# The second pass's activation blocks loaded from ScalarE's DMA queue instead of SyncE's

## The reference, cut to what matters

```python
mod = silu(c) @ ada_w + ada_b; shift, scale, gate = split(mod, 3)
h = rms_norm(x, norm_pre) * (1 + scale) + shift        # 1024 x 2048
q, k, v, z = h @ w_in                                  # 2048 x 8192, 8 heads x 256 columns each
p = softmax(mask(q k^T * scale))                       # two maps of 128 columns a head
attn = p[0] - lam * p[1]
o = rms_norm(attn @ v, subln) * (1 - lambda_init) * silu(z)
out = x + gate * rms_norm(o @ w_out, norm_post)
```

## Time and profile before

| | us |
|---|---|
| median of 3 runs | 2010.06 |
| lowest, highest | 2008.69, 2011.51 |
| the profiled execution's own time | 2007.15 |
| its span in the profile | 2005.2 |

### The profile page before, as it was taken

One profiled execution on the slowest core, in us unless ns is written; L12 is line 12 of the kernel. 1 busy time (PEld: TensorE's weight loads), 2 busy tenths in 40 slices (PEclk: granted clock), 3 DMA queues, 4 the chain that ended last, 5 costly groups with the idle time before them and its releaser, 6 DMA issues.

```text
span 2005.2 us, 26598 instructions
## 1 busy us (share of the span) xinstructions
PE 1940.0 (97%) x9252; PEld 1587.8 (79%) x9252; DVE 1277.7 (64%) x2096; ACT 785.8 (39%) x1567; POOL 566.1 (28%) x624
## 2 busy tenths in 40 slices
PE   3989999999999999999999999999999999999998
PEld 1358888888888887888888888888888878888886
DVE  1456766666655544787888888878888755434352
ACT  4433333333444332344444444444444433322240
POOL 1023333423365522433243423233242310000000
PEclk9999999999999999999999999999999999999999
DMA  9658666664365767786867778776867685476553
GB/s 301 208 179 263 211 191 216 199 203 141 134 213 197 260 243 262 231 243 201 254 207 231 229 222 255 211 238 201 253 208 242 213 291 169 132 255 200 161 154 85
DMA packets 391489, 426.52 MB, mean 213 GB/s; under 512 B 21078, under 2 KB 287420, under 8 KB 388796
## 3 DMA queue, kind: packets, MB, share of 16 engines
q1 hardware_dynamic: 391072, 424.76, 66.6%
q10 hardware_dynamic: 284, 0.05, 0.0%
HBM read 294.70 MB, written 130.03 MB: 212 GB/s over the span
## 4 chain that ended last, share of the span: by engine, by line
PE 90%; DVE 3%; issue 2%; DMA 2%; POOL 1%; ACT 1%; SPq 1%; DVEq 0%; POOLq 0%; ACTq 0%
PE ps L1544 28%; PE ps L1546 27%; PE ps L1545 27%; PE ps L1532 3%; PE ps L1664 2%; SPq L475 1%; PE ps L1638 1%; PE ps L1520 1%; POOL stg L736 1%; POOL sums L723 1%; DMA w_raw<-in_diff_w_out_dram 1%; PE ps L1683 1%; DVE ring L1109 1%; DMA h_dr<-stg 0%; DVE cc_low L1268 0%
## 5 line engine op out<-in xcount | busy, mean ns | idle before, releaser
L1544 PE MATMUL ps<-blk,ring 128*128 128x512 f32 x1536 | 608.7, 396 | 12.1 <-ACT cc L888 5.3
L1546 PE MATMUL ps<-blk,ring 128*128 128x512 f32 x1536 | 600.6, 391 | 0.0
L1545 PE MATMUL ps<-blk,ring 128*128 128x512 f32 x1536 | 600.5, 391 | 0.0
L1544 PEld LDWEIGHTS ps<-blk,ring 128*128 128x128 f32 x1536 | 289.8, 189 | 72.0 <-issue 13.5
L1546 PEld LDWEIGHTS ps<-blk,ring 128*128 128x128 f32 x1536 | 289.6, 189 | 61.7
L1545 PEld LDWEIGHTS ps<-blk,ring 128*128 128x128 f32 x1536 | 289.8, 189 | 57.1
L1109 DVE TENSOR_TENSOR ring<-sums,ring 128x512 fp32r<-128x512 f32 x256 | 225.4, 881 | 128.3 <-ACT ring L819 126.0
L723 POOL TENSOR_TENSOR sums<-raw 128x512 f32<-128x512 f32 x128 | 192.6, 1505 | 386.5 <-DVE ring L1109 287.0
L819 ACT ACTIVATE ring<-sums 128x512 fp32r<-128x512 f32 x256 | 160.0, 626 | 177.8 <-PE ps L1546 177.8
L1109 DVE TENSOR_TENSOR ring<-raw,ring 128x512 fp32r<-128x512 f32 x192 | 161.5, 842 | 83.4 <-ACT ring L819 82.5
L723 POOL TENSOR_TENSOR sums<-sums,raw 128x512 f32<-128x512 f32 x128 | 189.8, 1482 | 25.5 <-DVE ring L1109 18.4
(11 more groups left out here) (152 smaller groups left out, 3017.2 us busy)
## 6 DMA issues: line engine op xcount, KB each, us to landing
raw<-in_diff_w_in_dram SPq DMA_DIRECT2D x64, 1024.0 KB, 7.2
d_dr<-cc SPq DMA_DIRECT2D x128, 256.0 KB, 2.8
cc<-d_dr SPq DMA_DIRECT2D x128, 256.0 KB, 4.0
w_raw<-in_diff_w_out_dram SPq DMA_DIRECT2D x128, 256.0 KB, 3.6
ada<-in_ada_w_dram SPq DMA_DIRECT2D x108, 256.0 KB, 4.0
ada<-in_ada_w_dram SPq DMA_DIRECT2D x32, 512.0 KB
q_sb<-q_dr SPq DMA_DIRECT2D x64, 256.0 KB, 3.2
k_sb<-k_dr SPq DMA_DIRECT2D x64, 256.0 KB, 4.0
```

What stands on the lines that cost most here:

```text
L1544: MM(dst, a_hi, b_hi, start=start, stop=False, skip_group_check=True)
L1545: MM(dst, a_hi, b_lo, start=False, stop=False, skip_group_check=True)
L1546: return MM(dst, a_lo, b_hi, start=False, stop=stop, skip_group_check=True)
```

## The change

The seven `load_blk` calls move from SP's list into ACT's, at the same n, with the same waits and semaphores. In ACT's list they stand at the end of an iteration, behind `first_out(n - 1)` and `high_w(n + 3)`.

```diff
         @block.sync
-            def load_blk(op):
-
-                if op < 2:
-                    for e in range(2):
-                        sp.wait_ge(stg_st[e], 16 * 14)
-                    sp.wait_ge(xT_mm, 32)
-                else:
-                    sp.wait_ge(prod, NA - NP + op - 1)
-                sp.dma_start(slotB[op][:, :, :, :].bitcast(F32), h_dr[op]).then_inc(blk_in[op], 16)
             for n in range(NA):
...
-                if n in (NA - 22, NA - 20):
-                    load_blk((n - NA + 22) // 2)
-                if n > NA - 6:
-                    load_blk(n - NA + 7)
                 if NA - 3 <= n < NA - 1:
                     load_partial(GP, (C11, C12)[n - NA + 3])
...
         @block.scalar
+            def load_blk(op):
+
+                if op < 2:
+                    for e in range(2):
+                        act.wait_ge(stg_st[e], 16 * 14)
+                    act.wait_ge(xT_mm, 32)
+                else:
+                    act.wait_ge(prod, NA - NP + op - 1)
+                act.dma_start(slotB[op][:, :, :, :].bitcast(F32), h_dr[op]).then_inc(blk_in[op], 16)
+
             for n in range(NA):
...
                 if 0 <= j < 4 and 4 <= r < 4 + NP:
                     high_blk(j * NP + r - 4)
+                if n in (NA - 22, NA - 20):
+                    load_blk((n - NA + 22) // 2)
+                if n > NA - 6:
+                    load_blk(n - NA + 7)
```

## The result

The changed kernel takes 2013.76 us (median of 22 runs, 2010.17 to 2017.81), the one before 2009.38 (22 runs, 2006.03 to 2012.01). The ratio is 1.0022 with a 95% interval of 1.0016 to 1.0028: 4.4 us slower, just over the 0.2% that the prediction set as its bound for a change that can be told. The profiled execution took 2017.81 us with a span of 2015.6, which is 4 us over the median of its kind. That is 10.4 us more than the profiled execution of before: 2.1 us before product 224, 5.0 from product 224 to 230, and 3.3 behind it, of which 2.6 lie between 1600 and 1640 us, far from the change.

A forecast was written before the change was run, and what follows sets the result against it. TensorE, 97% busy, was taken to lose time only to waits and lowered clock at the turn of the passes. Packets one for one add 3.4 us to 2007.15: 2010.6, or 2013.5 on the median's scale; range 2006.4 to 2017.5.

The forecast's parts named there:

- What bounds the kernel: TensorE is busy 97%; at the turn of the passes late partials cost 4.85 us of waits and 3.4 of clock.
- Seven issues hidden on ACT: Seven block issues on ACT at 0.44 us each, 3.1 us in all, fit its idle time before splits.
- The start near 732.2: ACT issues block 2 behind the split at 731.50, 3.5 us later than SP's 728.72.
- Blocks 0 and 1 cost nothing: Issued 22 and 21 products before they are read, they cost nothing even if their loads take twice as long.
- SP is no longer held: C12's load can be issued near 740, not 744.9, seemingly gaining 5 us if the data then moves.
- Does it move?: Two queues on full DMA engines: bytes shared equally lands C12 near 744, packets one for one, the end taken, near 765.
- The other end: DMA engines share bytes equally between queues: SP's transfers get 212 GB/s and are through by 743.
- The sum: With packets one for one, C12 lands 764.8, product 228 starts 765.7, product 230 3.4 us later than before; chance 42%.
- rival 2: C22's load, behind stores and reads again, lands 4 us later: 3.5 us more, 2017.0; chance 20%.
- The first: Engines share by bytes, both waits go, product 230 waits for block 6: 2006.4 to 2008.1, say 2007.1; chance 22%.
- The third: ACT is held 7.9 us at blocks 5 and 6, as SP was: end 2014 to 2015; chance 6%.
- The fourth: A few small packets, say four, pass per large one; C12 near 757, within 2 us of before; chance 10%.

The follow-up runs named there:

- the first experiment: The changed kernel with blocks 2 to 6 back in SyncE's list, only blocks 0 and 1 issued by ScalarE; ratio to the kernel before 1.0002 (0.9992 to 1.0012).

## Why the prediction was right

*What bounds the kernel*: right. The cost that can be traced to the change appeared where a partial was late at the turn of the passes.

*Seven issues hidden on ACT*: right, 0.33 us each and no hold. The start near 732.2 was late by 0.7: with the 2.1 us of this execution taken off it was 731.5, since an issue goes out beside the split and not behind it.

*Blocks 0 and 1 cost nothing*: right, by the profile of the first experiment.

*SP is no longer held*: C12's load was issued at 742.3, not near 740, since product 218's store took 10.2 us to land beside the blocks. Nothing hung on it, for C12 stood behind raw.

*Does it move?* This was the choice that decided, and the end taken, packets one for one, holds: 271 to 272. The other end, bytes shared equally, is excluded by that row and by the runs of 4 KB. The evidence that the prediction had was thin: one instruction fetch of 0.99 us, which is less than 1.24 but also more than the 0.62 of a block's packet. It had to be set against other fetches: those of 16 KB on q8 in the trace of before take 0.88 us at the least and 1.02 in the median, so this one was hardly slowed. The prediction did not make that comparison, and one packet is little; in part it was luck. The Trainium skill's rule (DMA: Bandwidth & Descriptors, section Queues, rings and completion order), a round at packet granularity, agrees with the trace in that; its turns of some 9 to 17 descriptors do not, for a turn here was a single packet, by the 264 of 271 above. The same page's sentence that several issuing engines save only issue time (section Issuing engines are not separate DMA queues) did not hold here: the change also altered which transfers got through first, and that is what cost time.

*The sum*, with 2.1 us taken off: C12 landed at 766.1 where 764.8 was reckoned, 228 started at 767.0 (765.7), C22 was issued at 766.8 and landed 2.6 later (766.1 and 2.8), and the turn grew by 5.0 us in the profile, 4.4 in the medians, where 3.4 was forecast with 2.9 to 4.8 as the forecast's own range: the profile is just over it, the medians are in it. Two terms were undersized. C12 landed 1.3 us later: raw landed at 765.4, where its packets were reckoned to be through by 763.1. The sum took all 16 DMA engines alike. Of raw's 1024 packets 986 had started by 765.0, which is 762.9 and as reckoned, but the last ended at 767.2, and the landing followed that one; from 762.5 to 763.5 ten packets of blocks were still in the traffic. And 228 took 22.13 to 27.39 us of the turn, 5.26, at the lowered clock, not 4.57. Product 229 with its transposes took 3.34, which is 0.3 less than the 3.4 forecast implies. The chances put 55% on within 0.2% and 35% on slower; it came out slower, by a hair. The upper end of the whole range, 2017.5, is 0.5 above rival 2's own 2017.0; the prediction gives no reason for it.

*The rivals.* The first did not come. Nor did the second: C22 landed 2.6 us after issue; but its mechanism, C22 bound by the store ahead of it, appeared as soon as C12 was no longer late. The third did not come with 16 KB packets and did with 4 KB. The fourth is excluded by the packet counts.

## What to carry to other kernels

A second DMA queue was no faster lane here: beside a queue of large packets each small packet waited for one large one, so a load of many short runs crawled, and all behind it in its queue. Before moving a load, count packets and not bytes on each queue, and look at what is queued behind the smallest ones. Here the order inside one queue, critical partials first and each just ahead of the block it would have waited for, gave what the second queue was to give, 0.36%.

## What was not expected of the hardware

An issue is held by the number of packets waiting, it seems, and not by bytes: ScalarE issued the five blocks, 10.5 MB in 40 packets an engine, at 0.33 us an issue, and with the same bytes in 160 packets it was held for 5.00 and 7.49 us. Not all of them were waiting at once. Counting the packets issued and done in the traces, about 25 an engine were open after the last issue with 16 KB and 54 with 8 KB, both without a hold, and 99 with 4 KB when block 5's were counted in. SyncE was held for 5.28 us at 744.82 and for 10.94 at 750.62 in the changed kernel, each time with about 87 open, raw's 64 and partials of 8. The limit itself was not measured.
